# Ones times a high and a low fp32r part instead of one fp32 array, in the LayerNorm and the second RMSNorm of an encoder layer

## The reference

```python
def _rms(x, g, eps=1e-6):
    y = xf * lax.rsqrt(jnp.mean(xf * xf, axis=-1, keepdims=True) + eps); return y * g
def _layernorm(x, g, b, eps=1e-5):
    mu = jnp.mean(xf, axis=-1, keepdims=True)
    var = jnp.mean(jnp.square(xf - mu), axis=-1, keepdims=True)
    return (xf - mu) * lax.rsqrt(var + eps) * g + b
h = _rms(x, norm1_g); proj = h @ w_in                    # q, k, v and the gated conv input
attn = _window_attention(q, k, v, sink)                  # +-128 window, 8 heads, QK-norm, ALiBi
u = silu(_layernorm(_dwconv(a * sigmoid(gate), 31 taps)))   # 512 channels
x = x + concat(attn, u) @ w_out
h2 = _rms(x, norm2_g)                                    # 1024 channels
x = x + (silu(_dwconv3(h2 @ w_gate)) * (h2 @ w_up)) @ w_down    # hidden width 2816
```

## Time and profile before

| | before |
|---|---|
| median of 3 runs | 2663.15 us (2662.3 to 2664.71) |
| the profiled execution | 2662.67 us, its span 2660.9 us |
| granted TensorE clock | 0.998 |
| busy: PE, PEld, DVE, ACT, POOL | 2631.4, 2337.7, 1820.6, 1258.5, 192.8 us |
| instructions of DVE, of PE | 3020, 13191 |

### The profile page before, as it was taken

How to read it: one execution, slowest core, us unless ns; L and a number is a source line. 1 busy time by engine, 2 the same in 40 slices (tenths; PEclk the granted TensorE clock), 3 DMA queues, 4 the chain that set the end, 5 groups by cost and what they waited for, 6 DMA issues and landing times.

```text
span 2660.9 us, 35240 instructions
## 1 busy us (share of the span) xinstructions
PE 2631.4 (99%) x13191; PEld 2337.7 (88%) x13191; DVE 1820.6 (68%) x3020; ACT 1258.5 (47%) x2031; POOL 192.8 (7%) x332
## 2 busy tenths in 40 slices
PE   8999999999999999999999999999999999999998
PEld 6777777788889988889998889998899999999998
DVE  4775658787686876676876677876257576765764
ACT  6345464566454447345446345446144333533432
POOL 0110021100110000010000010000000000000001
PEclk9999999999999999999999999999999999999999
DMA  9967679633843444843443853433745521222211
GB/s 332 349 227 249 249 280 361 231 128 125 298 165 117 156 132 135 290 167 115 157 136 123 291 169 120 157 129 132 284 157 174 177 64 60 68 65 63 68 52 66
DMA packets 138761, 453.73 MB, mean 171 GB/s; under 512 B 24449, under 2 KB 37121, under 8 KB 121953
## 3 DMA queue, kind: packets, MB, share of 16 engines
q1 hardware_dynamic: 111616, 349.17, 39.0%
q0 software_dynamic: 26976, 102.32, 10.5%
HBM read 362.63 MB, written 88.79 MB: 170 GB/s over the span
## 4 chain that ended last, share of the span: by engine, by line
PE 93%; DVE 3%; issue 1%; DMA 1%; ACT 1%; SPq 0%; POOL 0%; DVEq 0%; ACTq 0%; POOLq 0%
PE bank L2131 31%; PE bank L2147 16%; PE bank L2277 12%; PE bank L2083 12%; PE bank L2117 8%; PE bank L2293 7%; PE bank L2231 2%; PE bank L2209 2%; PE bank L2220 2%; DMA wraw<-w_in_t 1%; DVE weights L1561 0%; PE bank L2176 0%; DMA weight_scratch<-weights 0%; ACT weights L1147 0%; ACT part_hi L1404 0%
## 5 line engine op out<-in xcount | busy, mean ns | idle before, releaser
L2131 PE MATMUL bank<-hw_hi,weights 128*128 128x440 f32 (+1 forms) x2816 | 812.2, 365 | 0.0
L2131 PEld LDWEIGHTS bank<-hw_hi,weights 128*128 128x128 f32 x2816 | 530.0, 188 | 47.9 <-issue 12.9
L2131 PE MATMUL bank<-hw_lo,weights 128*128 128x440 f32 (+1 forms) x1408 | 510.8, 363 | 0.0
L2147 PE MATMUL bank<-mid,weights 128*128 128x438 f32 x2112 | 431.9, 364 | 0.0
L1561 DVE TENSOR_TENSOR weights<-wraw,weights 128x1024 fp32r<-128x1024 f32 x286 | 348.8, 1220 | 117.0 <-ACT weights L1147 116.8
L2147 PEld LDWEIGHTS bank<-mid,weights 128*128 128x128 f32 x2112 | 396.0, 189 | 33.3 <-issue 7.6
L1147 ACT ACTIVATE weights<-wraw 128x1024 fp32r<-128x1024 f32 x286 | 301.5, 1054 | 256.9 <-DMA wraw<-w_down_t 171.2
L1668 DVE SCALAR_TENSOR_TENSOR cc<-win,par,cc 128x512 f32<-128x512 f32 x600 | 414.5, 744 | 0.0
L2083 PE MATMUL bank<-h_hi,weights 128*128 128x512 f32 x1104 | 358.6, 398 | 2.9 <-DVE weights L1561 2.9
L2131 PEld LDWEIGHTS bank<-hw_lo,weights 128*128 128x128 f32 x1408 | 264.4, 188 | 16.6 <-issue 1.0
L2083 PEld LDWEIGHTS bank<-h_hi,weights 128*128 128x128 f32 x1104 | 207.9, 188 | 56.0 <-issue 8.3
(11 more groups left out here) (213 smaller groups left out, 3688.0 us busy)
## 6 DMA issues: line engine op xcount, KB each, us to landing
weights<-weight_scratch SPq DMA_DIRECT2D x88, 1024.0 KB, 5.9
wraw<-w_ffn_t SPq DMA_DIRECT2D x176, 512.0 KB, 3.5
wraw<-w_down_t SPq DMA_DIRECT2D x88, 512.0 KB, 3.5
weight_scratch<-weights POOLq DMA_DIRECT2D x22, 1024.0 KB, 8.3
part_raw<-w_ffn_t SPq DMA_DIRECT2D x88, 256.0 KB, 2.6
part_raw<-w_pass_t SPq DMA_DIRECT2D x44, 256.0 KB, 2.6
cat_hi<-cat_scratch SPq DMA_DIRECT2D x10, 1024.0 KB, 6.6
cat_lo<-cat_scratch SPq DMA_DIRECT2D x10, 1024.0 KB, 9.0
```

The lines of the kernel that those rows point to most:

```text
L2131: mm = nc.tensor.matmul(out, l[:, k, :], r[:, k, 1:TC + 1] if s else r[:, k, :], start=(k == 0 and j == 0), stop=(k == KT - 1 and j == 2))
L2147: mm = nc.tensor.matmul(out, l[:, q, :], mid[:, k, part, :], start=(k == 0 and j == 0), stop=(k == FH - 1 and j == 2))
```

## The change

- After the last add, VectorE copies `ln_acc` to an fp32r tile `sum_hi` and writes `ln_acc - sum_hi` to an fp32r tile `sum_lo` (`split_sum`). TensorE waits for the second of the two and multiplies fp32r ones by `sum_hi` and by `sum_lo` into the same bank (`sum_parts`), in place of the one fp32 matmul. This holds for all three sums of all five chunks.
- `sum_lo` lies where `ln_acc` lies, `sum_hi` where `ln_st` lies. So there are waits of VectorE for work that it has done itself earlier: `scaled` (`ln_apply`), `s_h2` (`norm2_apply`), `centred`.
- `ones` becomes an fp32r tile: a memset of 128 columns of `ln_a` and a copy. `first_sum` reads it as fp32 and remains one fp32 matmul.
- The counts of the semaphores follow (`LN_ADDS`, `N2_ADDS`). The table `WORK`, the slots and the placing of the convolution stay.

```diff
@@ constants
+LN_ADDS, N2_ADDS = CT - 1 + 2, KT - 1 + 2
@@ encoder_layer
-        ones = sb("ones", [P, P])
+        ones = sb("ones", [P, P], F32R)
...
+        SUM_AT = R_SIDE + 2 * 4 * GROUP * BAND + 2 * 4 * AT * P + 4 * (TB + 2 * P) + 4 * (BLOCKS + 2) * KV_W + 4 * BAND + \
+            2 * up(4 * (TB + 2 * HALO)) + 4 * CT * TB
+        sum_lo, sum_hi = run(SUM_AT, ("sum_lo", [P, TB], F32R), ("sum_hi", [P, TB], F32R))
@@ VectorE
+            def split_sum(signal, n):
+                dve.wait_ge(signal, n)
+                nc.vector.tensor_copy(sum_hi[:], ln_acc[:]).then_inc(signal, 1)
+                dve.wait_ge(signal, n + 1)
+                nc.vector.tensor_tensor(sum_lo[:], ln_acc[:], sum_hi[:].bitcast(F32), ALU.subtract).then_inc(signal, 1)
...
             def ln_add(c):
...
+                if c > 0:
+                    dve.wait_ge(s_l["scaled"], c)
+                    dve.wait_ge(s_h2, KT * c)
+                split_sum(s_l["added"], LN_ADDS * c + CT - 1)
...
             def ln_add_squares(c, half):
...
+                    dve.wait_ge(s_l["centred"], c + 1)
+                    split_sum(s_l["sq_added"], n + CT - 1)
...
             def norm2_add(c, o):
...
+                if o == KT - 1:
+                    if c > 0:
+                        dve.wait_ge(s_h2, KT * c)
+                    dve.wait_ge(s_l["scaled"], c + 1)
+                    split_sum(s_n2a, n)
...
-            nc.vector.memset(ones[:], 1.0).then_inc(s_set, 1)
+            nc.vector.memset(ln_a[:, 0:P], 1.0).then_inc(s_set, 1)
+            dve.wait_ge(s_set, 4)
+            nc.vector.tensor_copy(ones[:], ln_a[:, 0:P]).then_inc(s_set, 1)
@@ TensorE
+            def sum_parts():
+                nc.tensor.matmul(bank[SHARE][:], ones[:], sum_hi[:], start=True, stop=False)
+                return nc.tensor.matmul(bank[SHARE][:], ones[:], sum_lo[:], start=False, stop=True)
...
             def ln_sum(c):
                 pe.wait_ge(s_shared, SHARED["ln_sum", c] - 1)
-                pe.wait_ge(s_l["added"], (CT - 1) * (c + 1))
-                nc.tensor.matmul(bank[SHARE][:], ones[:], ln_acc[:], start=True, stop=True).then_inc(s_l["sum"], 1)
+                pe.wait_ge(s_l["added"], LN_ADDS * (c + 1))
+                sum_parts().then_inc(s_l["sum"], 1)
```

More of the change, by code:

```diff
@@ L1312, in ln_squares @@
                 if half:
-                    act.wait_ge(s_l["sq_added"], (CT - 1) * c + 1)
+                    act.wait_ge(s_l["sq_added"], LN_ADDS * c + 1)
                 elif c > 0:
@@ L1335, in ln_swish @@
                 else:
-                    act.wait_ge(s_l["sq_added"], (CT - 1) * (c + 1))
+                    act.wait_ge(s_l["sq_added"], LN_ADDS * (c + 1))
                     act.wait_ge(s_l["var"], c + 1)
@@ L1344, in x2_square @@
                 if o >= 2:
-                    act.wait_ge(s_n2a, (KT - 1) * c + max(o - 2, 1))
+                    act.wait_ge(s_n2a, N2_ADDS * c + max(o - 2, 1))
                 elif c > 0:
-                    act.wait_ge(s_n2a, (KT - 1) * c)
+                    act.wait_ge(s_n2a, N2_ADDS * c)
                 nc.scalar.activation(sq[o % 2][:], x2[:, o, :], ACT.Square).then_inc(s_x2q, 1)
@@ L1676, in ln_add @@
                 for j in range(2, CT):
-                    dve.wait_ge(s_l["added"], (CT - 1) * c + j - 1)
+                    dve.wait_ge(s_l["added"], LN_ADDS * c + j - 1)
                     nc.vector.tensor_tensor(ln_acc[:], ln_acc[:], cc[:, j, :], ALU.add).then_inc(s_l["added"], 1)
+                if c > 0:
+                    dve.wait_ge(s_l["scaled"], c)
+                    dve.wait_ge(s_h2, KT * c)
+                split_sum(s_l["added"], LN_ADDS * c + CT - 1)
             def ln_centre(c):
@@ L1685, in ln_add_squares @@
             def ln_add_squares(c, half):
-                n = (CT - 1) * c
+                n = LN_ADDS * c
                 dve.wait_ge(s_l["squared"], CT * c + 2 * half + 2)
@@ L1761, in norm2_add @@
             def norm2_add(c, o):
-                n = (KT - 1) * c + o
+                n = N2_ADDS * c + o
                 dve.wait_ge(s_x2q, KT * c + o + 1)
@@ L1936, in _ @@
                                     slope[:, AT + HEADS:AT + 2 * HEADS], ALU.mult).then_inc(s_set, 1)
-            dve.wait_ge(s_set, 6)
+            dve.wait_ge(s_set, 7)
             for n in range(SLOTS + 1):
@@ L2164, in first_sum @@
                 pe.wait_ge(s_x0a, PIECES)
-                nc.tensor.matmul(bank[A_MISC][:], ones[:], x0_acc[:, 0, :], start=True, stop=True).then_inc(s_x0m, 1)
+                nc.tensor.matmul(bank[A_MISC][:], ones[:].bitcast(F32), x0_acc[:, 0, :], start=True, stop=True).then_inc(s_x0m, 1)
             def qk_sum(c):
@@ L2234, in values @@
                 mm.then_inc(s_pv, 1)
+            def sum_parts():
+                nc.tensor.matmul(bank[SHARE][:], ones[:], sum_hi[:], start=True, stop=False)
+                return nc.tensor.matmul(bank[SHARE][:], ones[:], sum_lo[:], start=False, stop=True)
             def ln_sum(c):
                 pe.wait_ge(s_shared, SHARED["ln_sum", c] - 1)
-                pe.wait_ge(s_l["added"], (CT - 1) * (c + 1))
-                nc.tensor.matmul(bank[SHARE][:], ones[:], ln_acc[:], start=True, stop=True).then_inc(s_l["sum"], 1)
+                pe.wait_ge(s_l["added"], LN_ADDS * (c + 1))
+                sum_parts().then_inc(s_l["sum"], 1)
             def ln_var(c):
                 pe.wait_ge(s_shared, SHARED["ln_var", c] - 1)
-                pe.wait_ge(s_l["sq_added"], (CT - 1) * (c + 1))
-                nc.tensor.matmul(bank[SHARE][:], ones[:], ln_acc[:], start=True, stop=True).then_inc(s_l["var"], 1)
+                pe.wait_ge(s_l["sq_added"], LN_ADDS * (c + 1))
+                sum_parts().then_inc(s_l["var"], 1)
             def norm2_sum(c):
                 pe.wait_ge(s_shared, SHARED["norm2", c] - 1)
-                pe.wait_ge(s_n2a, (KT - 1) * (c + 1))
-                nc.tensor.matmul(bank[SHARE][:], ones[:], n2_acc[:], start=True, stop=True).then_inc(s_n2m, 1)
+                pe.wait_ge(s_n2a, N2_ADDS * (c + 1))
+                sum_parts().then_inc(s_n2m, 1)
             def pair_product(k, q, g, p):
@@ L2298, in pair_down @@
                 mm.then_inc(s_used, 1)
-            pe.wait_ge(s_set, 4)
+            pe.wait_ge(s_set, 5)
             for n in range(SLOTS):
```

## The result

| | before | after |
|---|---|---|
| median of 7 runs | 2663.15 us (2661.26 to 2664.99) | 2671.66 us (2670.45 to 2674.67) |
| ratio, 95% interval | | 1.0028 [1.0018, 1.0037] |
| the profiled execution, its span | 2662.67, 2660.9 us | 2674.67, 2672.9 us |
| granted TensorE clock | 0.998 | 0.996 |

The change costs 8.5 us by the medians (7.5 by the ratio); +0.98 was forecast, and 2671.66 lies above the range. The two instructions on each engine cost what was forecast. What was missed lies in what TensorE does around them.

What follows compares the result with a forecast made beforehand. TensorE, busy 99% of the span, was taken as the bound. Nine free places (-3.6), three sums of squares (+2.06) and three of values (+2.52) gave +0.98 us: 2663.65 profiled, 2664.1 as a median, range 2660 to 2668.5.

Steps and rivals of the forecast that it cites:

- What TensorE saves: At each of 15 sums, an fp32r pair of 0.46 us replaces an fp32 matmul of 0.86: 0.40 us saved.
- What VectorE is given: At each sum, a copy of 0.42 us and a subtraction of 0.69, with gaps about 1.18 us of delay.
- its own earlier instructions: VectorE's added waits, for `scaled`, `s_h2` and `centred`, are passed already and nothing queues behind them: costed at nothing.
- Place by place: Nine free places give -3.6 us; three waiting sums of squares cost +2.06, three sums of values +2.52.
- The two tight places: Squares of chunk 2 (0.12 us to spare) and values of chunk 1: counted among the free places, no wait.
- What lies behind: VectorE's instructions behind a split, late by up to 1.18 us, are covered by slack before TensorE needs them: costed at nothing.
- the nine gains: Nine free places, among them all five of norm 2, each save 0.40 us on TensorE: -3.6 us.
- no DMA is issued otherwise: Across the kernel, no DMA is issued or moved by the change, so no cost was entered for it.
- the first (no wait shows): Rival: at all 15 places no wait shows, or later waits absorb the stalls: -6.0 us, 2657.1; chance 0.04.
- The second (VectorE's lateness reaches TensorE everywhere): Rival: behind the nine free splits TensorE meets late VectorE work: 10.7 us more, 2674.8; chance 0.04.
- The third: Rival: at the sums, the pair isn't shorter than the fp32 matmul: +5.6 us, 2669.7; chance 0.03.

Runs made afterwards that it cites:

- both_later2: both_later, but chunk 2's LayerNorm steps after the mean and its ln_var stay in their slots: 2662.59 us, 0.9995 of the kernel before.
- pe_half: Kernel before, with the last add writing fp32r and TensorE multiplying ones by it twice, no low part, no new VectorE instruction: 2661.31 us, 0.9989 of before.
- dve_half: Changed kernel with the split made and waited for, but one fp32 matmul of the unsplit sum: 2673.79 us, 1.0032 of before; second time 2676.84.
- both_later: Changed kernel, split behind the bias on VectorE, ln_sum of chunks 2 to 4, ln_var of 0, 2, 3, 4 one slot later: 2663.40 us, 0.9992 of before.

## Why the prediction was wrong

By its own steps:

- **What TensorE saves, 0.40 a place: right.** The pair's step shows as -0.35 to -0.40 at the places that have room, in every kernel with the pair. From the 4 passes for fp32 in the Trainium skill, "FP8 and Floating Point Precision", TensorE Precision Notes, the estimate was 0.43; the traces show 0.40 at most, as the step of 0.23 gives. (By that 0.43 the prediction's sum would have come out 0.4 us lower, not 0.5: by its own account the length counts at 12 places.)
- **What VectorE is given: right in the instructions, short in what stands around them.** 0.428 and 0.693 us. The Trainium skill, "VectorE: DVE Perf Modes", tier table, from which 0.43 was estimated for the copy, agrees with it. How 0.42 was reached, by taking two pointers' price off `tensor_scalar`, no run tests. But the step that the added waits of VectorE name "its own earlier instructions", "passed already", and cost "nothing" failed. The values of chunk 0 have one wait ahead of the copy, and it starts 0.03 us after the adds; with two waits the gap is 0.10, with three 0.13, at all 15 places in each of the three traces. Only one place has a single wait, and no run changed the number of waits at a place. The gap also needs an input that was just made: in both_later2, where the sum is long finished when the copy comes, three waits leave none (its copy at 1414.58 starts before the 0.16 us of the instruction ahead of it, at 1414.47, are over). Chunk 0 in the timeline of VectorE (adds end at 322.70), against the 0.13 shown for chunk 3:

```profile
321.28 1.42 DVE L1690 TENSOR_TENSOR ln_acc<-ln_acc,cc 128x512 f32<-128x512 f32 x2
322.73 0.43 DVE L1679 CAST sum_hi<-ln_acc 128x512 fp32r<-128x512 f32 x1
```

- **Place by place: the right six of fifteen, each sized 0.1 us short.** Values of chunks 2 to 4: +0.84, +1.12, +0.89 (forecast 0.73, 1.00, 0.79). Squares of chunks 3 and 4: +0.57, +0.87 (0.48, 0.79). These are the 0.07 to 0.10 of the waits. Squares of chunk 0: +0.99 (0.79), 0.07 of it the waits; for the rest the last add comes 0.12 us later against TensorE, which has gained 0.12 net at the sum before, and VectorE has not. In all 5.3 for 4.6. The two tight places did not wait.
- **"What lies behind … I cost it at nothing": failed.** Of the nine gains 1.7 us are given back at the next dependence: +0.28 at 337 us, +0.38 at 478 (a wait for a row maximum of 0.78 us before, now 1.16), +0.65 at 637, +0.37 at 1043. The step looked for VectorE's lateness there. pe_half shows three of the four without any: an engine that arrives earlier at something it already waits for, or reaches just in time, keeps nothing. Only 637 us needs the delay (0 in pe_half, 0.26 in dve_half, 0.65 with both).

With these the places make -3.5 + 5.3 + 1.7 = +3.5, not +0.98. That alone, 2666.6, would have been inside the range. Two terms were not in the sum at all:

- **TensorE's clock behind the stalls**, +1.6 in the mean. The granted clock by stretch (us, busy and records of PE, clock, DMA share, GB/s), values of chunk 3, after and then its third trace, in which it did not fall:

```profile
1410.00:1420.00 10.00, 8.41 (x38) 0.86 0.35 121
1420.00:1430.00 10.00, 10.00 (x50) 0.96 0.19 58
```

```profile
1410.00:1420.00 10.00, 8.42 (x45) 1.00 0.39 127
1420.00:1430.00 10.00, 10.00 (x52) 1.00 0.18 56
```

  The same busy time and the same stall. In eight traces with these stalls (values of chunks 3 and 4) the clock fell to 1.2 GHz behind 9 of 16, each time for 3.4 us, which costs 1.5 to 1.7 us. In the twelve traces without them it never fell there. In the six traces where these stalls last 1.4 to 1.6 us it fell behind 6 of 12, so at these two places a stall costs about 0.8 us more than its length, in the mean. But behind the other four places it never fell, although the stalls at the squares of chunks 0 and 4 are as long (1.4 to 1.6 us, 15 of them in these eight traces). So the length of a stall alone doesn't decide, and what does isn't shown.
- **The early stretch**, +2.9 in the mean, taken as unmoved since no DMA is issued otherwise. Its chain is shown, its cause is open. Part of it is the clock again: at half behind this wait in two of the three traces after, those with +4.2 and +4.3. The 2.0 us at 2140 to 2155 us, too, hold a fall of the clock. Two of the three traces after have them, none of the five before, but pe_half and one of dve_half do. They lie in a stage that the change doesn't touch, and their cause is open.

Of the rivals, the first (no wait shows) is what both_later nearly is. The second (VectorE's lateness reaches TensorE everywhere) happened at one place of nine, the values of chunk 1. The third is refuted by the steps of 0.23 and by the 0.40 that pe_half saves at 13 places. The mistake in the numbers was not a rival missed but a range that held only the two priced engines: it left out what a stall triggers and took every gain behind it as kept. Of the 8.9 us between the traces, 3.5 at the places and 1.6 of the clock are shown to come from the change; the early stretch and the one at 2140 us, 4.3 together, are located but not explained.

## What to carry to other kernels

Splitting an operand to spare TensorE time (here 0.40 us) can gain only where the consumer stands later than the split. So move the consumer, and put what else waits on the splitting engine (here the row maximum) ahead of the split: one move without the other cost as much as none. Count a shortening of the bounding engine only up to its next wait: here nearly half of the gains at places with room (1.7 of 3.5 us), and a third of those of TensorE's half alone (1.8 of 5.6), were given back. And allow in the range for more than a new stall's length, for what the clock may do behind it: here 0.8 us in the mean at two places, nothing at four.

## What the runs showed of the hardware

- A wait that is already passed is not always free on VectorE: ahead of the copy, one wait goes with a gap of 0.03 us to the instruction before, two with 0.10, three with 0.13 (15 places), where that instruction makes the copy's input. Where the input is long finished, three waits left no gap (both_later2).
- A stall of TensorE of 1.4 to 1.6 us is in some executions followed by 3.4 us at 1.2 GHz and in others not, in the same kernel at the same place (0.86 against 1.00 granted over 10 us). At two other places stalls as long were never followed by it (15 stalls).
- The same 320 KB load on POOL's queue, with the DMA engines 95% or more busy, took 7.4 to 11.2 us over 20 traces; TensorE lost up to 2.8 us by it, and up to 4.3 us where its clock fell behind the wait.
